# Multi-head latent attention in one kernel: score units, turnings and projections of three head pairs in one interleaved order, rotary halves as separate rows

## The reference, cut to what matters

```python
p = h @ w_in
q_c, kv_c, k_pe, gate = jnp.split(p, [384, 384 + 256, 384 + 256 + 32], axis=-1)
q = (rmsnorm_2(q_c, q_norm_g) @ w_qb).reshape(B, T, 16, 64 + 32)
kv = (rmsnorm_2(kv_c, kv_norm_g) @ w_kvb).reshape(B, T, 16, 64 + 64)
q_nope, q_pe = q[..., :64], q[..., 64:]
k_nope, v = kv[..., :64], kv[..., 64:]
# rotary part: q_pe and k_pe of the 512 tokens turned by cos, sin; k_pe is shared by all heads
s = jnp.einsum('bqhd,bkhd->bhqk', q, k) * (1.0 / math.sqrt(96))
o = jnp.einsum('bhqk,bkhd->bqhd', softmax(s), v)
d_x = (o * jax.nn.silu(g_x)) @ w_out
```

## Time and profile before

| | us |
|---|---|
| Median of 3 runs | 3272.67 (3271.75 to 3273.47) |
| The profiled execution's own time | 3273.59 |
| Its span | 3271.9 |
| PE busy | 2601.6 (80%) |
| VectorE busy | 1455.4 (44%) |
| ScalarE busy | 707.3 (22%) |
| POOL busy | 504.1 (15%) |
| Attention phase on PE, first projection to last weighted sum | 2830.8 to 3184.9 |

### The profile page before, as it was taken

How to read it: one execution, slowest core, us unless ns; L and a number is a source line. 1 busy time by engine, 2 the same in 40 slices (tenths; PEclk the granted TensorE clock), 3 DMA queues, 4 the chain that set the end, 5 groups by cost and what they waited for, 6 DMA issues and landing times. The chain is left out here.

```text
span 3271.9 us, 48852 instructions
## 1 busy us (share of the span) xinstructions
PE 2601.6 (80%) x19531; PEld 1508.1 (46%) x19531; DVE 1455.4 (44%) x2822; ACT 707.3 (22%) x1324; POOL 504.1 (15%) x465
## 2 busy tenths in 40 slices
PE   4998871977679999891499999588884869788877
PEld 2553340964334444340255564477773335344443
DVE  1542657542411111115778869545554720244431
ACT  2110330111101111110254511222221121133330
POOL 0000132300211111110000000211111300044440
PEclk8999876988789999995799899799996979899998
DMA  5212601011479999984344552334335511100002
GB/s 197 74 53 91 244 30 28 9 52 42 143 298 397 393 418 410 398 342 164 94 116 132 158 169 102 108 103 120 107 95 210 225 48 38 24 17 17 9 2 83
DMA packets 328822, 470.96 MB, mean 144 GB/s; under 512 B 151471, under 2 KB 225123, under 8 KB 303893
## 3 DMA queue, kind: packets, MB, share of 16 engines
q1 hardware_dynamic: 297157, 367.12, 32.6%
q10 hardware_dynamic: 17568, 75.51, 5.8%
q0 software_dynamic: 13872, 25.21, 2.1%
HBM read 413.68 MB, written 76.60 MB: 150 GB/s over the span
## 5 line engine op out<-in xcount | busy, mean ns | idle before, releaser
L1856 PE MATMUL psum<-ex_w,hT 128*64 128x512 f32 (+1 forms) x1104 | 330.8, 620 | 23.6 <-DMA ex_w<-in_exp_w_up 21.8
L1856 PEld LDWEIGHTS psum<-ex_w,hT 128*64 128x64 f32 (+1 forms) x1104 | 125.0, 159 | 223.4 <-issue 221.1
L3734 POOL TENSOR_SCALAR at_p<-at_p,at_stats 128x768 f32<-128x768 f32 x64 | 139.8, 2204 | 202.4 <-DVE at_stats L3759 202.4
L536 PE MATMUL psum<-hT,weights 128*128 128x512 f32 x384 | 166.8, 592 | 0.0
L1872 PE MATMUL psum<-ex_w,slot_act_t 128*64 128x512 f32 (+1 forms) x552 | 163.4, 597 | 1.4 <-DVE slot_act_t L2092 1.4
L2092 DVE COPY slot_act_t<-psum 128x256 f32<-128x256 f32 x45 | 19.1, 425 | 323.2 <-PE psum L1864 323.2
L481 PE MATMUL psum<-const,norm_xn 128*128 128x128 f32 x176 | 31.6, 345 | 123.8 <-DVE norm_xn L456 123.8
L1841 POOL DMA_INDIRECT scratch_ys<-slot_out,slot_row x45 | 45.7, 1015 | 463.0 <-issue 398.9
L3646 PE MATMUL psum<-mla_kT,at_qT 128*128 128x512 f32 (+1 forms) x256 | 94.7, 513 | 26.6 <-ACT at_p L3709 22.4
L2970 PE MATMUL psum<-rs_r_ident,rs_b 64*32 64x96 f32 x1536 | 89.2, 259 | 32.3 <-DVE rs_k_ident L3106 20.1
L536 PEld LDWEIGHTS psum<-hT,weights 128*128 128x128 f32 x384 | 73.0, 190 | 86.7 <-issue 86.1
(11 more groups left out here) (542 smaller groups left out, 5283.2 us busy)
## 6 DMA issues: line engine op xcount, KB each, us to landing
ex_w<-in_exp_w_gate SPq DMA_DIRECT2D x64, 1024.0 KB, 9.3
ex_w<-in_exp_w_up SPq DMA_DIRECT2D x64, 1024.0 KB, 18.3
ex_w<-in_exp_w_down ACTq DMA_DIRECT2D x60, 1024.0 KB, 10.1
mod_ring<-in_w_mod SPq DMA_DIRECT2D x12, 2048.0 KB, 13.7
scratch_features<-tokens SPq DMA_DIRECT2D x96, 256.0 KB, 3.8
weights<-in_w_in SPq DMA_DIRECT2D x6, 2048.0 KB, 7.9
mod_ring<-in_mod_w SPq DMA_DIRECT2D x6, 2048.0 KB, 10.2
ex_w<-scratch_ys SPq DMA_DIRECT2D x8, 1536.0 KB, 17.2
```

The costliest lines, as they stand in the source:

```text
L536: mm = pe.matmul(K.bank[2 * (f % 4)][:, :], K.wring[:, n % RING, k, m * P:(m + 1) * P], K.hT[:, k, TC:TT], start=(k == 0), stop=(k == KD - 1))
L1856: mm = pe.matmul(bank[at:at + n, :], XT[:, k, at:at + n], W[:, 0:2, k * DE:(k + 1) * DE], start=(k == 0), stop=(k == KD - 1))
L3734: pool.tensor_scalar(Pm[:, u, :], Pm[:, u, :], st[:, 3, u:u + 1], None, ALU.mult).then_inc(S["norm_done"], 1)
```

## The change

Score units, turnings and projections of three pairs are mixed. A round p has eight slots. Slot i holds score unit i of pair p + 1, then the turnings `TURNS[i]` of pair p (one or two of the twelve), then in slots 0, 2 and 4 the keys, values or queries of pair p + 2. After slot 7 comes the weighted sum of pair p. Rounds run from -2 to 7: round -2 has projections of pair 0 alone, round -1 the scores of pair 0 and projections of pair 1, round 6 no projections, round 7 turnings and the weighted sum alone. All engines follow the same order.

With it, turnings go through banks 4 and 5 by turns, projections through 6 and 7; turnings are numbered head by head instead of key tile by key tile; the probabilities have two buffers, the values three; the reciprocal of a unit stands one unit later in DVE's order, not two.

The rotary queries are one product: their weights are laid out as 32 columns and the 32 swapped ones below each other, so that one matmul group gives 128 rows (two heads). DVE multiplies the 64 rows of a head by a table of cosines over sines, with no sum. The rotary keys stand twice in `kT`, so that the score's contraction adds the two halves; the second copy is made by two DMAs from SP's queue in `mla_inputs`. No memset of `kT`, `qT` or `wpe` is left.

```diff
+        out[at + 32:at + 64, ROPE_COL:ROPE_COL + TX] = np.concatenate([-sin, sin])
...
+            for h, at in enumerate((NOPE, 0)):
+                sp.wait_ge(S["pe_out"], 4 * (h + 1))
+                sp.dma_start(kT[at + ROPE:at + 2 * ROPE, :, h, :], kT[at:at + ROPE, :, h, :]).then_inc(S["doubled"], 16)
+            sp.wait_ge(S["doubled"], 32)
...
-            pool.memset(kT[:, :, :, :], 0.0).then_inc(S["k_zero"], 1)
...
-            dve.wait_ge(S["k_zero"], 1)
...
-        wpe = buf("wpe", [P, 2, 2, NQ, QK])
+        wpe = buf("wpe", [P, 2, NQ, P])
         qT = buf("qT", [P, 2, 2, TX])
-        t = buf("rope", [P, 2, TX])
-        V = buf("v", [P, 2, NT, P])
-        Pm = buf("p", [P, 8, TT])
+        V = buf("v", [P, 3, NT, P])
+        Pm = buf("p", [P, 2, 8, TT])
         PT = buf("pT", [P, 2, NT, TX])
-        rope = (slice(NOPE, QK), slice(0, ROPE))
+        rope = (slice(HD, 2 * HD), slice(0, HD))
...
+        cosin = K.const[:, ROPE_COL:ROPE_COL + TX]
+        k_parts = ((6, 0, 512), (7, 512, TT))
+        TURNS = ((0,), (1, 2), (3,), (4, 5), (6,), (7, 8), (9, 10), (11,))
+        rounds = range(-2, PAIRS)
...
-                if p == 0:
-                    sp.wait_ge(S["wr_zero"], 1)
...
-                                          (wpe[:, s, 0, :, at:at + ROPE], NOPE, ROPE),
-                                          (wpe[:, s, 1, :, at:at + half], NOPE + half, half),
-                                          (wpe[:, s, 1, :, at + half:at + ROPE], NOPE, half)):
+                                          (wpe[:, s, :, at:at + ROPE], NOPE, ROPE),
+                                          (wpe[:, s, :, at + ROPE:at + ROPE + half], NOPE + half, half),
+                                          (wpe[:, s, :, at + ROPE + half:at + 2 * ROPE], NOPE, half)):
...
+            def keys(r):
+                s = r % 2
+                pe.wait_ge(wkv_in[s], 64 * (r // 2 + 1))
+                for n, (b, t0, t1) in enumerate(k_parts):
+                    if n == 0 and r:
+                        pe.wait_ge(S["qn_out"], 2 * r)
+                    if n == 1 and r:
+                        pe.wait_ge(S["rope_out"], 2 * r)
+                    if n == 1 and r >= 3:
+                        pe.wait_ge(S["o_out"], r - 2)
                     for k in range(NKV):
                         mm = pe.matmul(K.bank[b][:, 0:t1 - t0], wkv[:, s, k, 0, :], kvT[:, k, t0:t1],
                                        start=(k == 0), stop=(k == NKV - 1))
+                    mm.then_inc((S["k_a"], S["k_b"])[n], 1)
+
+            def values(r):
+                s = r % 2
+                for n, (b, j0, j1) in enumerate(((6, 0, 4), (7, 4, NT))):
+                    pe.wait_ge((S["k_a_out"], S["k_b_out"])[n], 2 * (r + 1))
+                    for j in range(j0, j1):
+                        for k in range(NKV):
+                            mm = pe.matmul(K.bank[b][:, (j - j0) * P:(j - j0 + 1) * P], kvT[:, k, j * P:(j + 1) * P],
+                                           wkv[:, s, k, 1, :], start=(k == 0), stop=(k == NKV - 1))
+                    mm.then_inc((S["v_a"], S["v_b"])[n], 1)
+
+            def queries(r):
+                s = r % 2
+                pe.wait_ge(wq_in[s], 128 * (r // 2 + 1))
+                pe.wait_ge(S["v_a_out"], r + 1)
                 for k in range(NQ):
+                    mm = pe.matmul(K.bank[6][:, :], wq[:, s, k, :], qcT[:, k, :], start=(k == 0), stop=(k == NQ - 1))
                 mm.then_inc(S["qn_mm"], 1)
+                pe.wait_ge(S["v_b_out"], r + 1)
+                for k in range(NQ):
+                    mm = pe.matmul(K.bank[7][:, :], wpe[:, s, k, :], qcT[:, k, :], start=(k == 0), stop=(k == NQ - 1))
                 mm.then_inc(S["qr_mm"], 1)
 
+            def score(q, u):
+                s, n = q % 2, 8 * q + u
+                h, qt = divmod(u, 4)
+                if u == 0:
+                    for name in ("k_a_out", "k_b_out", "qn_out", "rope_out"):
+                        pe.wait_ge(S[name], 2 * (q + 1))
+                if n >= 2:
+                    pe.wait_ge(S["exp_done"], n - 1)
+                for b, (t0, t1) in enumerate(((0, 512), (512, TT))):
+                    mm = pe.matmul(K.bank[2 * (u % 2) + b][:, 0:t1 - t0], qT[:, s, h, qt * P:(qt + 1) * P],
+                                   kT[:, s, h, t0:t1], start=True, stop=True)
+                mm.then_inc(S["sc_mm"], 1)
+
+            def turn(p, n):
+                h, kt = divmod(n, NT)
+                g = 2 * NT * p + n
+                if kt == 0:
+                    pe.wait_ge(S["norm_done"], 8 * p + 4 * (h + 1))
+                if g >= 2:
+                    pe.wait_ge((S["pt_a"], S["pt_b"])[g % 2], g // 2)
+                for qt in range(4):
+                    tr = pe.transpose(K.bank[4 + g % 2][:, qt * P:(qt + 1) * P],
+                                      Pm[:, p % 2, 4 * h + qt, kt * P:(kt + 1) * P], K.ident)
+                tr.then_inc(S["turned"], 1)
+
+            def weigh(p):
                 pe.wait_ge(S["pt_a"], NT * (p + 1))
                 pe.wait_ge(S["pt_b"], NT * (p + 1))
+                pe.wait_ge(S["v_a_out"], p + 1)
+                pe.wait_ge(S["v_b_out"], p + 1)
+                if p + 2 < PAIRS:
+                    pe.wait_ge(S["rope_out"], 2 * (p + 3))
+                else:
+                    pe.wait_ge(S["o_out"], p)
                 for kt in range(NT):
                     for h in range(2):
+                        mm = pe.matmul(K.bank[7][h * HD:(h + 1) * HD, :], V[:, p % 3, kt, h * HD:(h + 1) * HD],
                                        PT[:, h, kt, :], start=(kt == 0), stop=(kt == NT - 1))
                 mm.then_inc(S["o_mm"], 1)
 
+            for p in rounds:
+                for i in range(8):
+                    if 0 <= p + 1 < PAIRS:
+                        score(p + 1, i)
+                    if p >= 0:
+                        for n in TURNS[i]:
+                            turn(p, n)
+                    if p + 2 < PAIRS and i in (0, 2, 4):
+                        (keys, values, queries)[i // 2](p + 2)
+                if p >= 0:
+                    weigh(p)
...
+            def turned(p, n):
+                h, kt = divmod(n, NT)
+                g = 2 * NT * p + n
+                if n == 0 and p:
                     act.wait_ge(S["o_mm"], p)
+                act.wait_ge(S["turned"], g + 1)
+                act.activation(PT[:, h, kt, :], K.bank[4 + g % 2][:, :], ACT.Copy).then_inc(S["pt_a"], 1)
+
+            for p in rounds:
+                for i in range(8):
+                    if 0 <= p + 1 < PAIRS:
+                        exponentials(p + 1, i)
+                    if p >= 0:
+                        for n in TURNS[i]:
+                            if n % 2 == 0:
+                                turned(p, n)
+                    if p + 2 < PAIRS and i in (0, 2, 4):
+                        (keys, values, queries)[i // 2](p + 2)
...
-            pool.memset(qT[:, :, :, :], 0.0).then_inc(S["q_zero"], 1)
-            pool.memset(wpe[:, :, :, :, :], 0.0).then_inc(S["wr_zero"], 1)
...
+            def rotate(r):
+                if r >= 2:
+                    dve.wait_ge(S["sc_mm"], 8 * (r - 1))
+                dve.wait_ge(S["qr_mm"], r + 1)
                 for h in range(2):
+                    dve.tensor_tensor(qT[rope[h], r % 2, h, :], K.bank[7][rope[h], :], cosin[rope[h], :], ALU.mult)\
+                        .then_inc(S["rope_out"], 1)
             def inverse(n):
                 u = n % 8
                 dve.wait_ge(S["exp_done"], n + 1)
+                if n >= 8:
+                    dve.wait_ge(S["norm_done"], n - 7)
                 dve.reciprocal(st[:, 3, u:u + 1], st[:, 2, u:u + 1]).then_inc(S["inv_done"], 1)
+            def largest(q, u):
+                n, b = 8 * q + u, 2 * (u % 2)
+                dve.wait_ge(S["sc_mm"], n + 1)
+                dve.tensor_reduce(st[:, 0, u:u + 1], K.psum[:, b * 512:b * 512 + TT], AX.X, ALU.max)\
+                    .then_inc(S["max_done"], 1)
+                dve.wait_ge(S["max_done"], n + 1)
+                if n >= 8:
+                    dve.wait_ge(S["exp_done"], n - 7)
+                dve.tensor_scalar(st[:, 1, u:u + 1], st[:, 0, u:u + 1], -SCALE, None, ALU.mult).then_inc(S["nb_done"], 1)
+                if u:
+                    inverse(n - 1)
+
+            def turned(p, n):
+                h, kt = divmod(n, NT)
+                g = 2 * NT * p + n
+                if n == 1 and p:
                     dve.wait_ge(S["o_mm"], p)
+                dve.wait_ge(S["turned"], g + 1)
+                dve.tensor_copy(PT[:, h, kt, :], K.bank[4 + g % 2][:, :]).then_inc(S["pt_b"], 1)
+
+            for p in rounds:
+                for i in range(8):
+                    if 0 <= p + 1 < PAIRS:
+                        largest(p + 1, i)
+                    if p >= 0:
+                        for n in TURNS[i]:
+                            if n % 2:
+                                turned(p, n)
```

(69 more changed lines are left out.)

116 lines of the change are left out of this document (15 added, 101 removed).

## The result

The changed kernel takes 3194.79 us (median of 4, 3191.67 to 3197.48) against 3273.07 of the kernel before: **ratio 0.976, interval 0.9743 to 0.9777**. The profiled execution took 3196.45.

A forecast was written before the change was run, and what follows sets the result against it. PE, busy 80% of the span, was taken to bound the attention phase. The phase's parts gave 63.4 us less, minus 4 for switches and clock: 59.4 off the profiled 3273.6, so 3214 us, range 3205 to 3242.

The forecast's parts named there:

- the two allowances: Attention phase: 2 us for PE switching between transposes and score units, 2 us for a slower clock in round 7.
- the walk of the phase: Attention phase summed part by part, start through round 7: 290.6 us against 354.0 before, a difference of 63.4.
- Handoffs: PE's waits for copies behind a score unit's chain: 3.72 us after its start on VectorE, 4.57 on ScalarE.
- Work: PE's own work in a full round: 31.8 us instead of 34.4, with 1.345 per score unit.
- Two costs no row shows: PE's changes between transposes and score units, 0 to 7.8 us, and round 7's clock, 0 to 4.7; 2 taken for each.
- The Trainium skill's rule: Transposes do not count as PE being busy; by it round 7 pays 4.7 us, the forecast some 3 us later.
- Base: Starting time of the forecast: the profiled 3273.6 us, with nothing outside the attention phase changing.
- rotary products 1.4 us and hidden: Rotary multiply on VectorE: two products, about 1.4 us, free; at the old 4.17, 2.6 a round would come back.
- the end of the slow transposes: Two stretches of slow transposes in pairs 1 to 6 of the kernel before, 3.3 us, taken to vanish.
- B: Rival: late copies and score units delay each other in every round, up to 35 us over seven, say 3240; chance 0.16.
- C: Rival: short waits and transposes leave PE at half clock inside rounds, for half of their work 3309; chance 0.06.
- D: Rival: an unseen wait makes rounds serial and only removed work pays, 23 us, 3250; chance 0.06.

The follow-up runs named there:

- E6: Rolling order of rounds alone, with the old rotary queries of the kernel before: 3248.9 us, ratio 0.9951 against the kernel before.
- the repeat: The changed kernel, unaltered, measured again in a second session: 3197.0 us, ratio 0.9798 against the kernel before.
- E3: Changed kernel with only the copies put ahead of maximum (VectorE) and exponential (ScalarE), PE's order kept: 3189.71 us, ratio 0.976 to the kernel before.
- E4: Changed kernel with turning 11 moved from slot 7 to the end of slot 6: 3192.49 us, ratio 0.9775 to the kernel before.
- E2: Changed kernel with each slot's turnings ahead of its score unit on PE, ACT and DVE: 3185.7 us, in a second session 3181.06.
- E1: Kernel before with only the rotary part of the change, in the old order: 3218.88 us, ratio 0.985.

## Why the forecast was right in kind and wrong in size

The profiled execution came 3214.2 - 3196.45 = 17.8 us below the forecast. By the forecast's own steps: 4.0 are the two allowances, 7.6 the walk of the phase (290.6 against 282.98), 4.95 and 1.2 the stages ahead of and behind the phase. The phase alone takes the time to 3214.2 - 4.0 - 7.6 = 3202.6, already below the range. Of the 7.6 some 4.5 are handoffs.

- **Handoffs (the failed step: their price, not their mechanism).** "A copy that VectorE does behind the maximum and the reciprocal of a unit lets PE on 3.72 after that unit's start": measured 2926.32 - 2922.90 = 3.42. The maximum starts 1.50 after the unit, not 1.59; the copy follows the reciprocal's start by 0.08, where I had DVE free only at 2.88 and it was copying at 2.65. I had misread the row behind the 2.88: it is the start of the next unit's maximum, which waited for that unit on PE (1.40 + 1.50 = 2.90), not for DVE; PE goes on 0.10 after the copy, not 0.15. ScalarE's price was 4.57 and is 4.30 (2912.50 - 2908.20). So turnings 3 and 9 wait for nothing (0.14 each), turning 6 waits 0.85 (0.99), turning 10 0.40 (0.40), the weighted sum 1.68 (1.93): 2.93 a round instead of 3.6.
- **Work.** I took 1.345 for a unit, half of two back to back. A unit in a stream takes 1.29 and 1.40 right behind a weighted sum (2898.60 - 2897.20): the 2.69 held an extra 0.1 only once. 31.5 a round instead of 31.8. These two make 1.0 a round, less 0.36 in the longer one: 1.3 up to the first weighted sum, 5 x 35.4 - 172.5 = 4.5 over the full rounds, 1.2 in round 6; with 0.4 in round 7 and 0.2 at the start, the 7.6.
- **"Two costs no row shows", 2 each.** Both were nothing: the unit behind a turning takes the same 1.29, and the clock in round 7 was 1.00. The end of the range at no cost was the true one.
- **The Trainium skill's rule** ("TensorE: Matmul & The Clock Gate", Part 4, that transpose mode "doesn't count as PE-busy the same way") would have had round 7 at half clock. The trace disagrees again: 1.00 through its 48 transposes. E6's drop in its rounds came with transposes, but behind a stop of 2.45 us; no run here separates the two. Transposes are not needed for such a drop: behind the stop of 4.21 us ahead of the first score units the kernel before had a granted clock of 0.50 from 2851.3 to 2857.0, with matmuls alone.
- **Base.** "The change touches nothing else that takes time" holds (90.58 and 90.60 above), but the rest does not stand still: 3273.6 was one draw from stages that scatter by some 6 us, as the repeat shows. In its session the changed kernel gained 3264.4 - 3197.0 = 67.4, nearer to my 59.4 than the first 78. A range of 3205 to 3242 had nothing for that on its lower side, nor for both allowances and all waits being too dear together.
- **Right:** rotary products 1.4 us and hidden, no wait for a score bank or POOL, the three left-over waits in their places and order of size, the weighted sum's the worst (E3 removed the two of turnings, E4 that of the weighted sum, E2 the two and most of the third), 22 us to the second pair's scores, and the end of the slow transposes.
- **Rivals.** B (handoffs bind everywhere, 38 or more a round): no, the waits repeat and do not feed each other. C (clock): not here; but E6 shows it exists, at 1.7 us a round, when the old rotary work makes PE stand 2.45. D priced removed work alone at 23 us; E1 shows 47, since the wait behind that work and the clock's loss go with it in any order. Rotary halves, not the order, are two thirds of the gain or more (47.4 of 71.0 in the old order, 51.7 in the new).

## What to carry to other kernels

In an interleaved order, place a copy that frees a bank ahead of the new unit's chain: E3 did only that and shortened the phase by 9.2 us; E2, which also put the turnings ahead of the unit on PE, shortened it by 17.2. Price a step that follows another on the same engine from rows where the two stand back to back (0.08 from start to start for the small ones here), not from the time at which the engine was seen to be free. And where untouched stages scatter more than the term in question, judge by the phase's length, which here repeats to 0.04 us.

## What was unexpected of the hardware

- A stop of 2.45 us ahead of eight transposes cost more than itself: in E6 the granted clock fell to 0.50 just after PE resumed and was back at 1.00 from 2950.0, 1.73 us lost in the round shown. It happened in all five rounds (0.50 to 0.52 in a stretch of 1.8 or 2.0 us behind each such stop). The kernel before, with stops of 2.53 us at such a place, lost speed in two pairs of seven. What makes the difference was not found.
- The trace put the longest wait of the new rounds down to "issue". It was DVE's copy, as E4 shows.
- One program's scan ended 5.5 us apart in two executions at nearly the same mean clock (0.898 and 0.895). Its cause stays open.
